# A two-layer convolution and sparse-attention decode step: new convolution rows sent by GpSimd, denominators behind the first sums, value rows padded with zeros, the last product in two banks

## What is computed

```python
# layer A (conformer convolution)
a, b, z = split(rms_norm(x, g_pre) @ w_in, 3)              # 1024 -> 3072
glu  = a * sigmoid(b)
full = concat([conv_prev, glu])                            # 30 earlier rows; the last 30 of full are an output
c    = depthwise_conv(full, conv_w) + conv_b               # 31 taps
x1   = x + rms_norm((silu(layer_norm(c)) * silu(z)) @ w_out, g_post)
# shared keys and values of three branches, from rms_norm(x1) @ w_kv
kc, vc = compress(cmp rows)       # silu(chunks @ cmp_w1) @ cmp_w2, for the past and the new rows
ks, vs = slc rows (past pages and new rows);  kw, vw = state_win and new rows
# layer B (native sparse attention): 16 heads of 64 in 4 groups
q, zb, gate = rms_norm(x1) @ b_w_in
for branch in (cmp, slc, win):
    o[branch] = softmax(q k / 8 + bias) @ v
y   = sum over branches of gate * o * silu(zb)
out = x1 + rms_norm(y @ b_w_out, b_norm_post)
# further outputs: the last 30 rows of full (conv_prompt, conv_sample), the new k/v rows,
# and win_sample = state_win followed by the new rows
```

## Time and profile before

| | us |
|---|---|
| median of 3 runs (lowest, highest) | 876.87 (876.79, 877.28) |
| the profiled execution | 877.74 |
| its span | 875.9 |
| TensorE busy in the span | 848.3 (97%) |
| VectorE busy | 547.3 (62%) |
| ScalarE busy | 479.9 (55%) |
| GpSimd busy | 308.3 (35%) |

### The profile page before, as it was taken

The page is one execution under the profiler, slowest core; times in us unless marked ns, Lnnn a source line. Parts: engine busy times, 40 slices in busy tenths (PEclk is TensorE's granted clock), DMA queues, the critical chain, the costliest instruction groups (busy, mean ns, idle before and its releaser), DMA issues.

```text
span 875.9 us, 16465 instructions
## 1 busy us (share of the span) xinstructions
PE 848.3 (97%) x6202; PEld 759.9 (87%) x6202; DVE 547.3 (62%) x1179; ACT 479.9 (55%) x940; POOL 308.3 (35%) x311
## 2 busy tenths in 40 slices
PE   6999999999999999999988999999999999999996
PEld 4999999955888878889988999999999999987774
DVE  6479999998967693332255555656565645526674
ACT  6576777643742543233376666777667666624241
POOL 2389888879050000003032333333343433300000
PEclk9999999999999999999999999999999999999999
DMA  9456343217249455067321323332323322472621
GB/s 252 107 151 175 105 115 81 64 42 247 67 139 380 199 193 172 23 156 199 76 70 27 73 49 80 66 74 49 74 50 73 73 49 49 91 237 86 206 88 37
DMA packets 158164, 99.51 MB, mean 114 GB/s; under 512 B 97202, under 2 KB 147026, under 8 KB 158005
## 3 DMA queue, kind: packets, MB, share of 16 engines
q1 hardware_dynamic: 143278, 79.30, 33.7%
q0 software_dynamic: 4896, 10.32, 3.3%
q10 hardware_dynamic: 9911, 8.84, 3.1%
HBM read 89.58 MB, written 18.85 MB: 124 GB/s over the span
## 4 chain that ended last, share of the span: by engine, by line
PE 92%; DVE 3%; ACT 2%; ACTq 1%; issue 1%; POOL 0%; DVEq 0%
PE psum L2369 7%; PE psum L2370 7%; PE psum L2371 7%; PE psum L2003 6%; PE psum L2486 6%; PE psum L2004 6%; PE psum L2005 6%; PE psum L2082 5%; PE psum L2195 4%; PE psum L2446 4%; PE psum L2196 4%; PE psum L2197 4%; PE psum L2416 4%; PE psum L2402 3%; PE psum L1984 2%; PE psum L2558 2%
## 5 line engine op out<-in xcount | busy, mean ns | idle before, releaser
L842 ACT ACTIVATE arena<-psum 128x512 f32<-128x512 f32 (+7 forms) x211 | 92.1, 474 | 145.4 <-PE psum L2371 66.6
L2369 PE MATMUL psum<-u_hi,tile_hi 128*128 128x288 f32 x464 | 140.5, 303 | 0.0
L2370 PE MATMUL psum<-u_lo,tile_hi 128*128 128x288 f32 x464 | 137.6, 296 | 0.0
L823 POOL TENSOR_SCALAR arena<-arena,kept 128x512 f32<-128x512 f32 (+3 forms) x128 | 90.2, 725 | 134.0 <-DVE kept L1806 134.0
L2371 PE MATMUL psum<-u_hi,tile_lo 128*128 128x288 f32 x464 | 136.7, 295 | 0.0
L1468 DVE SCALAR_TENSOR_TENSOR psum<-arena,psum 128x512 f32<-128x512 f32 x168 | 127.0, 756 | 6.0
L2003 PE MATMUL psum<-h_hi,tile_hi 128*128 128x288 f32 x352 | 104.4, 297 | 0.0
L2004 PE MATMUL psum<-h_lo,tile_hi 128*128 128x288 f32 x352 | 104.2, 296 | 0.0
L2005 PE MATMUL psum<-h_hi,tile_lo 128*128 128x288 f32 x352 | 103.9, 295 | 0.0
L2369 PEld LDWEIGHTS psum<-u_hi,tile_hi 128*128 128x128 f32 x464 | 87.4, 188 | 3.0 <-issue 2.6
L2370 PEld LDWEIGHTS psum<-u_lo,tile_hi 128*128 128x128 f32 x464 | 87.4, 188 | 0.3
(11 more groups left out here) (330 smaller groups left out, 1887.4 us busy)
## 6 DMA issues: line engine op xcount, KB each, us to landing
tile_whole<-in_b_w_in SPq DMA_DIRECT2D x64, 256.0 KB
tile_whole<-in_a_w_in SPq DMA_DIRECT2D x24, 512.0 KB
arena<-in_cmp_w SPq DMA_DIRECT2D x4, 2048.0 KB, 9.9
kvw_whole<-in_w_kv SPq DMA_DIRECT2D x6, 1024.0 KB, 14.1
bias_copies<-bias_line POOLq DMA_DIRECT2D x4, 1280.0 KB, 23.6
arena<-in_x_prompt SPq DMA_DIRECT2D x8, 512.0 KB, 6.4
kvw_whole<-in_a_w_out SPq DMA_DIRECT2D x4, 1024.0 KB, 11.5
arena<-bias_copies SPq DMA_DIRECT2D x16, 256.0 KB, 3.8
```

What stands on the lines that cost most here:

```text
L823: pool.tensor_scalar(L, L, rden[:, 8 + j:9 + j], gR[:, i, h:h + 1], ALU.mult, ALU.mult).then_inc(S["pn_ready"], 1)
L842: return nc.scalar.activation(out, in_, ACT.Copy, scale=scale)
L2369: pe.matmul(pb(b, HT), w_hi, u_hi[:, k, here], start=(k == 0), stop=False)
L2370: pe.matmul(pb(b, HT), w_hi, u_lo[:, k, here], start=False, stop=False)
```

## The change

Eight edits:

- `squares`: the product `ones x squares` stands after ten of 16 products of `compress`, not six.
- The transposes of the new convolution rows stand ahead of TensorE's wait for the silus (`hid_ready`), and go to banks 2 and 3.
- The eight transfers of new convolution rows are issued by GpSimd behind its two large ones, and count on `late`. VectorE's wait before the first `kvh_whole` is for `co_out` 16 and for `late` 16 x (2 + 8).
- ScalarE loads the table of the exponential between `z_copy(0)` and `z_copy(1)`.
- `den_of_cmp(0)` stands behind `sums(0)`.
- In steps of the first branch `y_product(m, 0)` stands ahead of `next_lo`.
- `vnew` and `pts` have 128 rows, lie over the old `u_hi`, and are zeroed once by GpSimd behind the last weight tile; the value product of the new rows takes 128 rows of weights. The first four `new_v_rows` are issued earlier. The first two parts of `last_part` stand behind the first transposes of the sample loop.
- The first branch sum of the sample rows is formed one round earlier, the last product fills bank 4 and then bank 5 with a square for each, and the scale by `gpost_s` is taken out of the last two instructions of VectorE.

```diff
@@ SyncE
+            sp.wait_ge(S["zeroes"], ZEROED["rest"])
+            for n in range(4):
+                new_v_rows(n)
             sp.wait_ge(S["x1_out"], 16 * TT)
...
                 if n >= 4:
                     past_rows(n)
-                new_v_rows(n)
+                    new_v_rows(n)
@@ GpSimd
             pool.dma_start(O["win_sample"][:, 0:PAST], I["state_win"]).then_inc(S["late"], 16)
 
+            pool.wait_ge(S["co_ready"], 2)
+            for b in range(DB):
+                pool.dma_start(O["conv_sample"][0, b, W - 1 - DS:W - 1], conv_out_s[DS * b:DS * b + DS]).then_inc(S["late"], 16)
             pool.wait_ge(S["x1_out"], 16 * TT)
...
+            pool.wait_ge(S["tile_mm"], tile_done(N_TILES - 1))
+            pool.wait_ge(S["t_done"], turned_cmp(KD - 1))
+            pool.memset(vnew, 0.0).then_inc(S["zeroes"], 1)
+            pool.memset(pts, 0.0).then_inc(S["zeroes"], 1)
             y_sum(N_STEPS - 1)
@@ ScalarE
-            copy(conv_out_s[0:NS], pb(6, D, p1=NS)).then_inc(S["co_ready"], 1)
-            act.wait_ge(S["co_ready"], 2)
-            for b in range(DB):
-                act.dma_start(O["conv_sample"][0, b, W - 1 - DS:W - 1], conv_out_s[DS * b:DS * b + DS]).then_inc(S["co_out"], 16)
-
+            copy(conv_out_s[0:NS], pb(2, D, p1=NS)).then_inc(S["co_ready"], 1)
...
-            for n in range(2):
-                z_copy(n, 2 + 4 * n)
+            z_copy(0, 2)
+            nc.scalar.activation(sd[:, 6:7], ident[:, 0:1], ACT.Exp)
+            z_copy(1, 6)
@@ VectorE
                     if k == 0:
                         dve.wait_ge(S["y_ready"], KD)
-                        dve.wait_ge(S["co_out"], 16 * (1 + DB))
+                        dve.wait_ge(S["co_out"], 16)
+                        dve.wait_ge(S["late"], 16 * (2 + DB))
...
             sums_cmp(0)
-            den_of_cmp(0)
             for n in range(N_STEPS):
                 m, br = n // 2, 1 + n % 2
                 sums(n)
+                if n == 0:
+                    den_of_cmp(0)
...
-                next_lo(tile_over(n, 1))
                 if br == 1:
                     y_product(m, 0)
-                elif m + 1 < KD:
+                next_lo(tile_over(n, 1))
+                if br == 2 and m + 1 < KD:
...
-            dve.wait_ge(fy_out[0], 16 * 2)
             dve.wait_ge(x_in[0], 16 * 6)
-            link(dve, V.scalar_tensor_tensor(out=y_out[:, 0, 0:D // 2], in0=pb(4, D // 2), scalar=rs[:, 4:5], in1=gpost_s,
-                                             op0=ALU.mult, op1=ALU.mult))
-            V.tensor_tensor(out=y_out[:, 0, 0:D // 2], in0=y_out[:, 0, 0:D // 2], in1=x1_back[:, 0, 0:D // 2],
-                            op=ALU.add).then_inc(S["fy"], 1)
+            V.scalar_tensor_tensor(out=y_out[:, 0, 0:D // 2], in0=y_out[:, 0, 0:D // 2], scalar=rs[:, 4:5],
+                                   in1=x1_back[:, 0, 0:D // 2], op0=ALU.mult, op1=ALU.add).then_inc(S["fy"], 1)
@@ TensorE
-                    if squares and j == 6:
+                    if squares and j == 10:
...
-            for h in halves_at[0]:
-                last_part(4 + h // 2, range(4 * (h % 2), 4 * (h % 2) + 4))
...
-                            weights = pts[:, n % 2, j, rows_p] if j < 2 else pts[0:DS, n % 2, 2, rows_p]
+                            weights = pts[:, n % 2, j, rows_p]
...
-                        ins = pe.matmul(pb(4, 2, CH, p0=half * NS, p1=half * NS + NS)[:, c], yT[:, k, SEQ:NT],
+                        ins = pe.matmul(pb(4 + c, CH, p0=half * NS, p1=half * NS + NS), yT[:, k, SEQ:NT],
                                         chunk_sb(C_OB + 2 * half + c)[:, k], start=(k == 0), stop=(k == KD - 1))
+                ins.then_inc(S["fo_mm"], 1)
```

More of the change, by code:

```diff
@@ L298, in build @@
             """.split()}
-        ZEROED = {"slot": 1, "blocks": 3, "bias": 4, "pad": 5, "probs": 6, "table": 7, "queries": 8}
+        ZEROED = {"slot": 1, "blocks": 3, "bias": 4, "pad": 5, "probs": 6, "table": 7, "queries": 8, "rest": 10}
         w_in = [sem(f"w_in{i}") for i in range(RING)]
@@ L1364, in _ @@
             act.wait_ge(fy_out[1], 16 * 2)
-            act.wait_ge(S["co_out"], 16 * (1 + DB))
-            act.wait_ge(S["late"], 16 * (2 + 2 * DB))
+            act.wait_ge(S["co_out"], 16)
+            act.wait_ge(S["late"], 16 * (2 + 3 * DB))
         @block.vector
@@ L1735, in _ @@
             dve.wait_ge(S["kv_out"], KV_OUT)
-            dve.wait_ge(S["late"], 16 * (2 + 2 * DB))
+            dve.wait_ge(S["late"], 16 * (2 + 3 * DB))
             dve.wait_ge(S["gate_out"], 16)
@@ L1909, in _, with y_sample_sum @@
                 V.tensor_tensor(out=fold[:, half * NS:half * NS + NS], in0=ident[:, 0:NS], in1=ident[:, NS:P], op=ALU.add).then_inc(S["ones_ready"], 1)
+            def y_sample_sum(br):
+                ys = yT[:, :, SEQ:NT]
+                dve.wait_ge(S["ys_mul"], 2 * (3 * DB - 1 + br))
+                if br:
+                    dve.wait_ge(S["y_s"], 1)
+                V.tensor_tensor(out=ys, in0=ys, in1=y_br[:, br], op=ALU.add).then_inc(S["y_s"], 1)
             for w in range(2 * DB + 4):
@@ L1956, in _ @@
                     last_sum(norm_at[w - 2])
-            dve.wait_ge(S["ys_mul"], 2 * DB * 3)
-            ys = yT[:, :, SEQ:NT]
-            for br in range(2):
-                V.tensor_tensor(out=ys, in0=ys, in1=y_br[:, br], op=ALU.add).then_inc(S["y_s"], 1)
-                dve.wait_ge(S["y_s"], br + 1)
+                if w == 2 * DB + 2:
+                    y_sample_sum(0)
+            y_sample_sum(1)
             last_mean(3)
@@ L1964, in _ @@
             last_sum(3)
-            dve.wait_ge(S["fo_mm"], TT + 1)
-            V.tensor_scalar(ms[:, 4:5], pb(5, 1), 1.0 / D, EPS, ALU.mult, ALU.add).then_inc(S["ms_a"], 1)
+            dve.wait_ge(fy_out[0], 16 * 2)
+            for c in range(2):
+                dve.wait_ge(S["sq_a"], 2 * TT + c)
+                n_dve[0] += 1
+                V.tensor_tensor(out=y_out[:, 0, c * CH:(c + 1) * CH], in0=pb(4 + c, CH), in1=gpost_s[:, c * CH:(c + 1) * CH],
+                                op=ALU.mult).then_inc(dve_step, 1)
+            dve.wait_ge(S["fo_mm"], TT + 2)
+            V.tensor_scalar(ms[:, 4:5], pb(3, 1), 1.0 / D, EPS, ALU.mult, ALU.add).then_inc(S["ms_a"], 1)
             dve.wait_ge(S["sd_a"], 2 * TT)
             link(dve, V.reciprocal(rs[:, 4:5], sd[:, 4:5]))
-            dve.wait_ge(fy_out[0], 16 * 2)
             dve.wait_ge(x_in[0], 16 * 6)
-            link(dve, V.scalar_tensor_tensor(out=y_out[:, 0, 0:D // 2], in0=pb(4, D // 2), scalar=rs[:, 4:5], in1=gpost_s,
-                                             op0=ALU.mult, op1=ALU.mult))
-            V.tensor_tensor(out=y_out[:, 0, 0:D // 2], in0=y_out[:, 0, 0:D // 2], in1=x1_back[:, 0, 0:D // 2],
-                            op=ALU.add).then_inc(S["fy"], 1)
+            V.scalar_tensor_tensor(out=y_out[:, 0, 0:D // 2], in0=y_out[:, 0, 0:D // 2], scalar=rs[:, 4:5],
+                                   in1=x1_back[:, 0, 0:D // 2], op0=ALU.mult, op1=ALU.add).then_inc(S["fy"], 1)
         @block.tensor
@@ L2157, in _ @@
                 compress(1, ht, slice(16, 33), w1_far).then_inc(S["cs_mm"], 1)
+            pe.wait_ge(S["new_packed"], DB)
+            for k in range(KD):
+                ins = pe.transpose(pb(2, KD, P, p1=NS)[:, k], new_rows[:, k], ident)
+            ins.then_inc(S["co_tr"], 1)
             pe.wait_ge(S["hid_ready"], 4)
@@ L2535, in _ @@
                     pe.transpose(pb(3, P), orow[:, n % 2], ident).then_inc(S["ot_tr"], 1)
-                for h in halves_at.get(w, ()) if 0 < w < 2 * DB else ():
+                for h in halves_at.get(w, ()) if w < 2 * DB else ():
                     last_part(4 + h // 2, range(4 * (h % 2), 4 * (h % 2) + 4))
```

25 lines of the change are left out of this document (13 added, 12 removed).

## The result

The changed kernel takes 885.13 us (median of 4 runs, 884.23 to 885.96) against 877.02 us (4 runs, 876.79 to 877.28): ratio 1.009, 95% interval 1.0078 to 1.0102. It is 8.1 us slower; 6.2 were forecast (883.1 us, range 878.5 to 888). The profiled execution took 885.12 us, its span is 883.3 us, 7.4 us longer than before; of the rest up to 8.1, 0.7 us is that before's profiled execution lay above its median.

What follows compares the result with a forecast made beforehand. TensorE, working in 97% of the span, was taken as the bound. With the early -3.3 swallowed, 15.4 - 4.5 - 2.4 - 0.8 - 1.5 = +6.2 us gave 883.1 us for the median, range 878.5 to 888.

Steps and rivals of the forecast that it cites:

- The first step: Before 290 us: three small TensorE waits go, about -3.3 us, none of which survives VectorE's new wait.
- The stall: VectorE's new wait before `kvh_whole` for GpSimd's transfers makes TensorE's `turn_b(2)` late: +15.4 us, ends +12.2 and +17.5.
- the landing of the eight behind the large transfer: Small transfers land 1.0 us behind the large one's 300.3 (ends 0 and 3.1); VectorE goes on at 301.3.
- The clock: After some 15 us idle at VectorE's new wait, TensorE restarts at a lower clock, costing 2.9 us.
- VectorE's floor: VectorE's chain takes 12.83 us from one `xn_b` to the next, so `turn_b(2)` is at least 13.2 us late.
- Small transfers wait only for their turn: On GpSimd's queue, the eight small transfers, issued long before, wait just for those in front; 1.0 us was added.
- The attention: Start of the prompt attention: earlier sums and scaling, no wait before `values(0)`; -4.5 us, or -2.8 if the clock drops.
- Sample loop: 128-row weights save a 0.15 us pause in each of 16 rounds, -2.4; reordered first transposes and `last_part`, -0.8 us.
- the end: At the kernel's end, a sum, a VectorE instruction and half a square go: -1.5 us, ends -0.8 and -1.8.
- No stall: Rival at VectorE's new wait: the transfers are through by 283 us, so nothing waits; 864.4 us, chance 0.08.
- A short stall: Rival: the large transfer lands some 5 us earlier, quick restart; term +8 to +10, 876 to 879 us, chance 0.06.
- A longer stall: Rival: small transfers land well behind the large one, or a later gain is missing; 887 to 892 us, chance 0.06.

Runs made afterwards that it cites:

- experiment 7: The change with the eight small transfers issued ahead of GpSimd's two large ones, on a semaphore of their own that VectorE waits for: 863.88 us, ratio 0.9845.
- experiment 5: The change with the `state_win` transfer cut to the first half of every sequence's rows, the rest left unwritten: 875.16 us, ratio 0.9977.
- experiment 6: The change with the `state_win` transfer split into two, rows 0 to 127 and 128 to 255 of all sequences, nothing left out: 879.91 us, ratio 1.0029.
- experiment 8: The change with 140 unused products of the identity with itself put ahead of `turn_b(1)` to fill TensorE's gap: 894.18 us, ratio 1.0193.
- experiment 9: The change with 80 unused products of the identity with itself put ahead of `turn_b(1)` to fill TensorE's gap: 885.48 us, ratio 1.0102.
- experiment 12: The kernel of experiment 7 with the compressed branch's denominators ahead of the first sums again: 864.43 us, ratio 0.987.
- experiment 11: The kernel of experiment 7 with the compressed branch's product behind the low part again in every step: 865.49 us, ratio 0.988.
- experiment 2: The kernel before, with only the eight transfers moved behind GpSimd's two large ones and VectorE waiting for all ten: 896.6 us, ratio 1.0217.
- experiment 10: The kernel of experiment 7 with 8-row weights and 8 rows of values again in the product with the new value rows: 865.99 us, ratio 0.9887.
- experiment 1: The change with the eight transfers issued by ScalarE again and VectorE waiting for those alone: 864.95 us, ratio 0.9855.
- experiment 3: The change with the `state_win` transfer cut to the first half of the sequences, the other half left unwritten: 884.5 us, ratio 1.0076.
- experiment 4: The change with the eight transfers in the same queue place but on a semaphore of their own that VectorE waits for: 885.24 us, ratio 1.0092.

## Why the prediction was right, and where it was not

**The first step** (three small waits, -3.3): right. They came to -3.6 in the change and were swallowed, as said; with the stall away TensorE had 3.3 us of them at `turn_b(1)` (experiment 7, whose trace was 0.3 us behind before's at 120 us).

**The stall** (+15.4, measured +16.7): the mechanism is right and was shown from both sides: without it 864.95 us, alone 896.6. The term that was mis-sized is the landing of the eight behind the large transfer, "I add 1.0 us". VectorE was released at 302.8, 2.5 us behind the 300.3 of the earlier trace rows, near the upper end that had been kept (3.1). From the end of the last large packet to the release it was 2.6 us in the change and 3.2 us in experiments 5 and 6. The clock was sized nearly right: the stretch grew by 2.65 us where 2.9 was put, all of it by the clock (experiments 8 and 9). VectorE's floor stood as forecast, 12.82 us from `xn_b` to `xn_b` where 12.83 was put, and was not what bound.

**"Small transfers wait only for their turn"**: right in the result, not in the picture. In the change their data did not wait; the sign that they were done did (in experiment 6 both were late). And the release does not go by the ten MB in front of them: leaving out 2 MB of the 4 made a difference of 0.6 us or of 10, according to which 2.

**The attention** (-4.5, measured -4.3): the sum is right, its parts are not. Taken apart: the table load, costed at nothing, about 1.1 us (by subtraction); the denominators, costed at 1.2, 0.3 us (experiment 12); the product, 1.1 us in the chain that is left (experiment 11). That the sum came out so close, with one part four times too large and another left out, is luck in part. The remaining 1.7 to 1.8 us are the granted clock's drop at 464 us, here absent. Which wait brings the drop stays open. Experiment 11 has the wait of 2.85 us without it; before has a wait of 2.76 us 12 us ahead as well, and fell only behind the second; experiment 2 has the same two waits and fell behind each. So the 1.7 us are a gain of these traces, not one that the order of the code assures.

**Sample loop** (-2.4 and -0.8; measured -2.3 and -1.0) and **the end** (-1.5; measured -0.7 and -1.0): right, the loop's term shown by experiment 10. By the Trainium skill (TensorE: Matmul & The Clock Gate, "LDWEIGHTS (loading the stationary operand)"), weighed there, it would have been nought. What that section says of a load's own time agrees with the rows of experiment 10, where four loads of 128 rows took 0.20 us and four of 8 rows 0.19; the 0.17 us lie between loads of different form. The end's was read from the trace and not tested by a run of its own; so was the cost of the two memsets, 2.1 us of GpSimd's time for which TensorE shows no wait.

**The rivals.** "No stall" was priced at 864.4; experiments 1 and 7 give 864.95 and 863.88 for it. Its price was right, and its condition (the increments there by 283 us) was not met. The rule of the Trainium skill that spoke for it (DMA: Bandwidth & Descriptors, "Anatomy of one DMA — SWDGE (gpsimd) path": 2.0 us plus bytes at 436 GB/s, by which the queue's ten MB are estimated at about 25 us) doesn't hold for this transfer, which ran on half of the engines, in 64 KB pieces one behind the other, and landed after some 45 us. "A short stall" is what experiments 5 and 6 had, by other edits. "A longer stall" had the cause right that made the term 1.3 us dearer: the small ones were reported 2.5 us behind the large one. It was too small for the 887 us put on it.

## What to carry to other kernels

A small transfer that somebody will wait for must not stand behind a large one on GpSimd's queue, even if its data would go through other DMA engines: put it first (21 us here for moving three lines up), or on another queue. When a wait is replaced by one on a counter that others use too, the new wait is for the last of them, and its price is read from that one's landing. And a table load counts as hidden only if the instruction behind it isn't the one that somebody waits for: look at who waits for that instruction, not at the engine's idle time.

## What the runs showed of the hardware that was not expected

- How long a copy between two places in device memory takes went by its shape: 4 MB as 8 pieces of 512 KB kept 8 DMA engines busy (share 0.49, 213 GB/s); 2 MB as 4 pieces took as long (0.23, 99 GB/s); 2 MB as 8 pieces ended 10.6 us earlier (300.2 against 289.6).
- Eight transfers of 32 KB had their data in place by 285 to 287 us and were reported complete at 302 to 303 (the change, experiments 3 and 4); half of their increments came by 287.6 us, the other half from 296.2 on (experiment 4).
- TensorE's granted clock fell behind waits of 2.76 and 2.85 us (experiment 2) and of 1.96 us (experiment 9), and did not fall behind another of 2.85 us (experiment 11).
- VectorE's release varied by 2.9 us between kernels that issue the same transfers (301.83 in experiment 8, 304.69 in the ninth), more than most of the terms in the sum. Behind such a wait, distances between rows compare better than medians.
- An fp32 product of a 128 x 128 matrix went as two matmuls at 0.112 us each (31.43 us for 280), where a transpose of the same size is one.
